# RWKV scan: the products of levels 0 to 4 of a triangular inversion, made from 32x32 tiles of the array in place of 64x64 ones

## The reference, cut to what matters

```python
def step(S, inp):
    r_t, w_t, k_t, v_t, kk_t, a_t = inp
    sa = jnp.einsum('bhij,bhj->bhi', S, -kk_t)
    S = (S * w_t[:, :, None, :] + sa[..., None] * (kk_t * a_t)[:, :, None, :]
         + v_t[..., None] * k_t[:, :, None, :])
    y = jnp.einsum('bhij,bhj->bhi', S, r_t)
    return S, y
```

## Time and profile before

| what | value |
|---|---|
| median of 3 runs | 3879.78 us (3878.91 to 3880.33) |
| profiled execution | 3884.69 us, its span 3882.9 us |
| TensorE (PE) busy | 3568.8 us, 92% |
| VectorE (DVE) busy | 1858.4 us, 48% |
| ScalarE (ACT) busy | 909.3 us, 23% |
| the scan, first `solve` to last `solve` | 1672.96 to 2099.80 us of the span, 19 steps |
| instructions fetched for TensorE over the whole program (queue q8) | 151 packets, 2.47 MB |

### The profile page before, as it was taken

How to read it: one execution, slowest core, us unless ns; L and a number is a source line. 1 busy time by engine, 2 the same in 40 slices (tenths; PEclk the granted TensorE clock), 3 DMA queues, 4 the chain that set the end, 5 groups by cost and what they waited for, 6 DMA issues and landing times. The chain is left out here.

```text
span 3882.9 us, 67820 instructions
## 1 busy us (share of the span) xinstructions
PE 3568.8 (92%) x28504; PEld 3038.0 (78%) x28504; DVE 1858.4 (48%) x2745; ACT 909.3 (23%) x1332; POOL 179.9 (5%) x336
## 2 busy tenths in 40 slices
PE   8999999999799982899999899878969999999997
PEld 7888888887677871889887677667858888888885
DVE  5445445445566207656556344213164444544546
ACT  2111111111343215433334622213031111111112
POOL 0000000000000000522221000000000000000000
PEclk9999999999899995999999999889989999999998
DMA  3101100100235421133333330010010100100101
GB/s 124 39 32 34 47 32 32 49 22 12 101 97 147 133 79 65 37 89 83 82 85 126 103 125 16 33 44 22 22 44 33 49 32 32 49 32 32 46 8 54
DMA packets 86026, 225.74 MB, mean 58 GB/s; under 512 B 6736, under 2 KB 53456, under 8 KB 79824
## 3 DMA queue, kind: packets, MB, share of 16 engines
q1 hardware_dynamic: 81808, 210.91, 17.0%
q10 hardware_dynamic: 4032, 12.06, 0.8%
HBM read 176.07 MB, written 46.87 MB: 57 GB/s over the span
## 5 line engine op out<-in xcount | busy, mean ns | idle before, releaser
L289 DVE TENSOR_TENSOR main_acc<-main_acc,ffn_psum 128x512 f32<-128x512 f32 (+1 forms) x1056 | 617.6, 598 | 853.4 <-PE ffn_psum L205 852.8
L194 PE MATMUL ffn_psum<-x_xh,ffn_wi_h 128*128 128x512 f32 (+1 forms) x2112 | 525.5, 357 | 30.3 <-DVE ffn_wi_l L278 18.4
L194 PE MATMUL ffn_psum<-x_xh,ffn_wi_l 128*128 128x512 f32 (+1 forms) x2112 | 525.1, 357 | 0.0
L194 PE MATMUL ffn_psum<-x_xl,ffn_wi_h 128*128 128x512 f32 (+1 forms) x2112 | 525.0, 357 | 0.0
L194 PEld LDWEIGHTS ffn_psum<-x_xh,ffn_wi_h 128*128 128x128 f32 x2112 | 372.8, 188 | 98.2 <-DVE ffn_wi_l L278 18.8
L194 PEld LDWEIGHTS ffn_psum<-x_xh,ffn_wi_l 128*128 128x128 f32 x2112 | 349.9, 188 | 60.5
L194 PEld LDWEIGHTS ffn_psum<-x_xl,ffn_wi_h 128*128 128x128 f32 x2112 | 349.4, 188 | 61.2
L205 PE MATMUL ffn_psum<-ffn_hid_h,ffn_wo_h 128*128 128x512 f32 (+1 forms) x1056 | 380.5, 360 | 12.4 <-DVE ffn_hid_l L297 10.0
L205 PE MATMUL ffn_psum<-ffn_hid_h,ffn_wo_l 128*128 128x512 f32 (+1 forms) x1056 | 377.8, 358 | 0.0
L205 PE MATMUL ffn_psum<-ffn_hid_l,ffn_wo_h 128*128 128x512 f32 (+1 forms) x1056 | 376.7, 357 | 0.0
L249 ACT CAST ffn_hid_h<-ffn_hid 128x1280 fp32r<-128x1280 f32 x44 | 55.7, 1265 | 1066.0 <-DVE ffn_hid L295 1066.0
(11 more groups left out here) (297 smaller groups left out, 5324.0 us busy)
## 6 DMA issues: line engine op xcount, KB each, us to landing
ffn_w_raw_in<-ffn_w_in_dram SPq DMA_DIRECT2D x44, 1024.0 KB, 6.7
rws_pack<-pack SPq DMA_DIRECT2D x160, 225.0 KB, 2.6
ffn_w_raw_out<-ffn_w_out_dram SPq DMA_DIRECT2D x44, 512.0 KB, 3.7
mixin_w_raw<-mix_w_in_dram SPq DMA_DIRECT2D x27, 512.0 KB, 3.7
pack<-mixin_pack SPq DMA_DIRECT2D x4, 2580.0 KB, 15.5
fin_raw<-ca_w_kv_dram SPq DMA_DIRECT2D x16, 512.0 KB, 3.9
pack<-mixin_pack SPq DMA_DIRECT2D x4, 1920.0 KB, 12.3
proj<-mixin_low ACTq DMA_DIRECT2D x12, 640.0 KB, 3.0
```

The costliest lines, as they stand in the source:

```text
L194: mm = nc.tensor.matmul(ps[:, at + c * BANK:at + c * BANK + tn], w[:, slot, cols], x[:, k, t0:t0 + tn], start=(k == 0 and j == 0), stop=(k ...
L289: nc.vector.tensor_tensor(acc[:, o, t0:t0 + tn], acc[:, o, t0:t0 + tn], ps[:, at:at + tn], ALU.add).then_inc(added, 1)
```

## The change

Each of the 8 products of a direction at levels 0 to 4 was one of 64x64 by 64 columns. The transposed factor has nothing outside its two 32x32 blocks on the diagonal at these levels, so each product is now two, on the 32-row halves: the half `i = d` with all 64 columns, and the other half with only its own 32 columns. Nothing else changes, neither waits nor signals; the signal still hangs on the last product that is issued.

```diff
                     for q in QS:
-                        for s in HEADS:
-                            mm = nc.tensor.matmul(left(RL[d])[own(s), q], n_t[d][own(s), q], now_r[own(s), q],
-                                                  start=False, stop=True, skip_group_check=True)
+                        for i, cols in ((d, slice(0, C)), (1 - d, part(1 - d))):
+                            for s in HEADS:
+                                mm = nc.tensor.matmul(left(RL[d])[quadrant(s, i), q, cols], n_t[d][quadrant(s, i), q, part(i)],
+                                                      now_r[quadrant(s, i), q, cols], start=False, stop=True, skip_group_check=True)
                     mm.then_inc(raised[d], 1)
```

## The result

The kernel after takes 3957.8 us (median of 4 runs, 3938.7 to 3960.7), the kernel before 3880.1 us beside it (3878.9 to 3886.8): a ratio of 1.0186, 95% interval [1.0152, 1.0221], taken over all the runs (the two medians alone give 1.0200). The forecast was 3928 us, in a range of 3886 to 3968, and slower. The profiled execution took 3960.71 us, of which 3958.9 are the span. Nearly all of the loss is in the scan. The first row is the page's line for the changed products, as the earlier trace rows; the second its line for the weight loads.

A forecast was written before the change was run, and what follows sets the result against it. TensorE was taken to bound a clean step, with instruction fetches as a second limit behind it. Fetch-bound steps gave 473.5 us against 426.8, +46.7, plus 1.5 outside: 3933 profiled, 3928 us as median, range 3886 to 3968.

The forecast's parts named there:

- The products: Levels 0 to 4: both halves run side by side, 0.46 us a direction; 0.14 us saved at level 1.
- The halves take turns: Rival, chance 0.12: halves at levels 0 to 4 run in turn, 0.21 us more a direction; 3956 us.
- Changes of tile: Between 64-row and 32-row work: 12 changes a step, eight on the path, 1.05 us, less 0.14 saved.
- Code: TensorE in the scan: 320 more records a step, fetched in batches of 251 at 3.9 us each; chance 0.62.
- 6.3 + 20.2 - 1.0 = 25.5 us: Scan step with `turn_v`: `solve` to `score_k`, plus fetching 5.17 batches for the rest, less the time fetched ahead.
- the lead of 1.0 us: From `solve` to `score_k`, slow code at 5.0 us a batch lets fetches get about 1.0 us ahead.
- the one sum for the whole rest of the step: After `score_k`: 1297 records, 5.17 batches, 20.2 us of fetching against 16.7 us of PE work; the longer counts.
- The loads: Scan input loads: steps of 24.5 us outlast their chain, so the late load's 4.7 us PE wait goes.
- The chain's 22.5 us a step: Input loads in the scan, each issued when the one before has landed, take about 22.5 us a step.
- The last term: Ahead of the first `solve` and behind the last, one more inversion where PE mostly waits: +1.5 us.
- Only the tile changes count: Rival, chance 0.18: code comes faster when asked for faster, so steps gain only 0.9 us; about 3891 us.
- Not slower: Rival, chance 0.08: diagonal quarters need no draining, directions overlap wholly, code comes in time; 3875 us.

The follow-up runs named there:

- long halves alone: Kernel after with the 32-column half of each product at levels 0 to 4 left out; 3891.9 us, 1.0044.
- the pair of doses: Kernel after with the 32-column halves issued at levels 0 and 1 only (3901.3 us), and at levels 2 to 4 only (3934.4 us).
- the one with levels 0 and 1: Kernel after with the 32-column halves issued at levels 0 and 1 only; 3901.3 us, 1.0062.
- The kernel with narrow products: Kernel after with 8 columns in every matmul of the changed line in place of 64 and 32; 3979.9 us, 1.0269.
- With small loads: Kernel after with input loads of 8 columns in place of 450 from the third chunk on; 3935.1 us, 1.0156.
- the kernel after with loads not waited for: Kernel after with a step's input loads issued one behind the other without waiting for each to land; 3961.0 us, 1.0214.
- the kernel before with small loads: Kernel before with input loads of 8 columns in place of 450 from the third chunk on; 3870.1 us, 0.9979.
- the two meant for it: Kernel before with four, or two, unused semaphore increments behind each product call of levels 0 to 4; 4798.7 us and 4294.4 us.

## Why the prediction was right in its sign, and 30 us short

Of the 29.8 us between 3928 and 3957.8, 20.6 lie in the 19 steps (494.1 against 473.5), 7.2 outside them (8.7 against 1.5), and 2.0 in the median, which stands 2.9 us below the profiled execution and not 4.9.

(1) *The products: right.* The halves run beside each other: 0.42 us a direction, 0.46 forecast. Level 1 gave 0.17 us where I took 0.14. "The halves take turns", at 3956 the rival closest to the measured time, is refuted by the timeline; its time was right by chance. The 25 ns from start to start of the Trainium skill (TensorE: Matmul & The Clock Gate, "Wait — 56ns, not 53.3ns?") does not hold for these tiles: 63 steps in 0.74 us are 12 ns. One reading of rows was wrong and nothing hung on it: 127.2 of 401.8 us are about a third of TensorE's time in the scan, not a fifth.

(2) *Changes of tile: right.* 0.15 us from the last start of the products to the unit products; 0.73 us a clean step with the long halves alone, where the prediction had 0.9.

(3) *Code: the right mechanism, mis-sized.* Gaps 251 records apart that end when a packet has landed, 24 more packets, +62 us with the short halves. The step that failed is the sentence that a clean step is "6.3 + 20.2 - 1.0 = 25.5 us", 24.5 without `turn_v`, with 3.9 us a batch throughout. Measured are 25.94 and 25.02. The size of a batch was nearly right: those that TensorE waited for took 4.0 us in the mean. What did not hold are the lead of 1.0 us and the one sum for the whole rest of the step. In the row 1806.47 to 1827.05 four batches and most of a fifth pass without a gap for code, 4.12 us each with the gap of 1.30 at the end, set in the main by TensorE's own pace. Five packets belong to them, started at 1807.56, 1811.15, 1816.21, 1819.91 and 1824.63, so the one that the gap waited for was not fetched ahead in the slow part. Only the dense end of the step runs at the pace of fetches. The same is seen in the pair of doses: 128 records in the slow part cost 9 us, 192 in the dense part 42. How the miss divides between batch size, lead and sum was not worked out. Too low by half a microsecond a step, it costs 8 x 0.44 + 10 x 0.52 - 0.7 in the last step = 8.0 us of the 20.6 by which 494.1 exceeds 473.5.

(4) *What was not there: the clock.* I had written that a clock well under 1.00 would be something not reckoned with. Had all 19 steps been as the clean ones they would have taken 8 x 25.94 + 10 x 25.02 + 23.8 = 481.5 us. The other 12.6 us are in the ten steps (not counting the last) with a clock below 1.00. Each of the ten falls of this kernel begins in a gap or within 2 us behind one, but not each gap brings one: the 1.90 us ahead of 1806.47 did not. The kernel with long halves alone and the one with levels 0 and 1 have no such stretch in their steps. That the gaps cause the falls is not shown. The kernel with narrow products had fewer of them (38, 40 us in all, against 49 and 48.6 us) and the lower clock, 0.81. How much of the 12.6 us is the clock itself, and how much longer gaps in the same steps, was not taken apart either.

(5) *The loads: half right.* The late load of the kernel before did go: no wait of ScalarE for a load is left among its longest. The chain's 22.5 us a step does not follow from its row, though: 345.3 us / 137 waits are 2.5 us a load, 20 us for eight. And input loads cost the kernel after time in another way, which I had not priced. With small loads the 19 steps take 472.3 us, close to my 473.5, and the clock hardly falls: so loads lie behind most of both parts of the miss. Most of what they add to a batch is a later start of its packet (1.5 us after the restart against 1.3); whether it is the loads' packets or their bytes that delay it stays open. The last term, +1.5 us outside the steps, was +8.7. Of this 4.5 lie ahead of the first `solve`, which came at 1677.5 us, against 1673.0 in the kernel before; but it came at 1672.2 in the kernel after with loads not waited for and at 1675.3 in the kernel before with small loads, so most of it can be scatter. The rest was not traced.

"Only the tile changes count" (3891) was the result of the kernel with long halves alone and not of this one: code did not come faster for being asked for faster. "Not slower" fell with it. That the gaps are waits for code rests on the 251 records, on the doses and on the packets, behind whose landing every gap ends; a kernel that adds code alone is missing, because the two meant for it added something else.

## What to carry to other kernels

Count instructions as well as busy time where a program is written out straight: here a batch of 251 matmuls and weight loads that TensorE waited for came every 4.0 us with the input loads and every 3.7 with small ones, never under 3.1, so a run of matmuls that take less than about 30 ns each with their load is paid for in gaps. Smaller tiles cost least where slow code lies next to them (9 us for 128 records against 42 for 192). Look at the granted clock as well: the steps in which it fell account for 12.6 of the 494 us, and what made it fall stays open. A model that adds up the whole step and takes the larger of two sums is too kind: take the larger stretch by stretch.

## What the runs showed of the hardware that was not expected

- Four 32x32 tiles of two independent directions overlap: 64 matmuls started over 0.74 us, 12 ns each.
- Code for TensorE came in packets of 16.4 KB on a queue of its own, and slow work ahead of a dense part did not bring them earlier. Where they were the bound, a batch took 4.0 us from restart to restart, of which the packet itself took 1.1.
- Increments of a semaphore between matmuls cost about 0.14 us each: 4 of them to a product made the kernel 24% slower, with a granted clock of 0.61 in the scan.
- A kernel with 8 columns in place of 64 and 32 ran 22 us longer than the one with all of them, at a granted clock of 0.81 in the scan against 0.96.
- Small input loads made even the kernel before 0.2% faster. One late load (a wait of 4.7 us) is part of it; the waits for code fell as well, from 7.4 to 2.9 us, at a DMA share of 0.08 in place of 0.32.
